# Chunk stores on GpSimd's queue, a first maximum pass over four banks, six x tiles turned among the sample batches, and a finer wait ahead of the feed-forward

## The chip, the cores and the metric

The kernel runs on one core of one Trainium2 chip. The metric is the device time of one execution in microseconds (us). The core has five engines with queues of their own: TensorE (PE: matmuls and transposes), VectorE (DVE), ScalarE (ACT), GpSimd (POOL) and SyncE (SP, which here only issues DMAs). They meet through semaphores.

## The reference

One layer over 1024 prompt tokens and 8 sample batches of 16 tokens (T = 1152 tokens in all), float32:

```python
D_MODEL, SEQ, DEC_BATCH, DEC_SEQ, PAST_LEN = 1024, 1024, 8, 16, 256
H_A, DH_A, H_B, DK_B, DV_B, D_FF, CONV_W, PLE_DIM = 8, 64, 4, 128, 256, 2816, 3, 256
def trunk_layer(x, p, fox_past, ...):
    qa, ka, va, fa, qb, kb, vb, rb, a1, ga, gb = split(x @ w_in)
    logf = log_sigmoid(fa + b_fgate)
    ya = fox(qa, ka, va, cumsum(logf), fox_past) @ w_a_out       # causal softmax attention, 8 heads
    la = log_sigmoid(a1 @ w_a2 + b_a2) / 16
    ob, S = gated_linear_attention(qb * DK_B**-0.5, kb, vb, la, S0)       # 4 heads
    yb = (rms_norm(ob) * g_gla * silu(rb)) @ w_b_out
    x1 = layer_norm(ALPHA * x + (sigmoid(ga) * ya + sigmoid(gb) * yb) @ w_o)
    val, gate = split(causal_conv3(x1 @ w_up))
    x2 = layer_norm(ALPHA * x1 + (val * gelu(gate)) @ w_down)
    return layer_norm(ALPHA * x2 + (p @ w_pl) * sigmoid(x2 @ w_plg)), ka, va, logf, S, conv_new
```

The sample batches attend to their 256 past keys and values and to their own 16 tokens.

## The kernel before

All large products are exact to about float32: each operand is split into a rounded part (`_hi`, by ACT) and a rest (`_lo`, by DVE), and a product is three matmuls (`split3`). Code is written out per engine; the order on each queue is that of the code. The stages that the change touches, in order of time:

**Projection.** x is transposed by TensorE into `xh`/`xl` (keys `("xT", n)`, nine tiles of 128 tokens), and q, k and v of branch A are computed. Weights pass through a ring of four slots (`load` on SP, `split_hi`, `split_lo`). Chunks 12 to 15 are the first four of branch B: `qb`, `kb` and two of `rb`, of head 0. Memory of `xh`/`xl` is then reused by branch A, so x has to be loaded and transposed again for branch B (`xs2`, keys `("xT2", n)`, `x_again`, `x_hi`, `x_lo`).

**Branch A, prompt.** Each of 8 heads has a first pass, `row_scores` and `row_max` (12 row blocks: scores by TensorE, maximum by DVE's reduction), then `join_max`, a transpose `turn_max` and ACT's `max_row`, which put the row maximum into an operand. The second pass has 6 slots a head (t counts them: 6 h + s): `scores(t)`, ACT's exp and rounding, DVE's `probs_lo`, and `probs_v(t - 2)` on TensorE. The first pass of head h + 1 runs among slots 0 to 3 of head h, `turn_max(h + 1)` in slot 4; only head 0's stands alone. The first pass has two half banks of PSUM (`n % 2`). Operands of a head are put together by 8 DMAs from SP (`head_operands`, 256 KB most of them), in three sets. A head gives two output chunks: ACT's `chunk_out(h, c)` copies one from PSUM to the single tile `ost`, `store_chunk(h, c)` writes it (`branch_a`, 128 KB) and the row sums (`row_sums`, 2 KB) to DRAM, and the next `chunk_out` waits until both have landed. In the queues of before, `store_chunk` is SP's, in order with `head_operands`, the loads of past keys and values (`past`) and `x_again`. POOL scales finished pairs of heads: `row_sums`, `row_scales`, `load_pair`, `store_pair` (a 128x1024 multiply).

**Branch A, samples.** For b in 0 to 10 TensorE does `past_keys(b + 1)`, `sample_out(b - 3)`, `sample_scores(b)`, `sample_turn(b - 1)` and `sample_v(b - 2)`. PSUM is handed out in turn by `take`: four buffers, and each use waits until the use four places earlier is drained. Then come the nine `xT2` transposes, and branch B with `thirds(("qb", 0), ...)`: 3 products (g = 0, 1, 2) over 384 tokens each, 24 matmuls a product.

**Ahead of the feed-forward.** The products with `w_o` (L924) alternate with transposes of finished x1 tiles (`turn_x1`, L912). DVE does for each tile the residual (`add_x`), `stats`, `centred`, `x1_scaled`, and `x1_lo`, which drains the PSUM buffer of the transpose. TensorE then waits at

```python
            copied(pe, ("wo", 1, NT - 1), ("x1T", NT - 3))
```

and starts `first_chunk`: six products of `w_up`, with `turn_x1(7)` and `turn_x1(8)` between them.

Of the kernel before, what the change touches and what calls it, by code (L numbers as in the profile page):

```python
# [24 lines left out]
P = 128  # L25
# [63 lines left out]
def build(nc, x_prompt, x_sample, cache_fox_k, cache_fox_v, cache_fox_logf, state_gla, cache_ffn_conv,  # L89
# [4 lines left out]
    with ctx:  # L94
# [121 lines left out]
        def x_tile(x, n):  # L216
# [21 lines left out]
        xs2 = [at(off["va"] + 1024 * i, 1024) for i in range(4)] + [at(off["kT"] + T * i, 1024) for i in range(4)] \  # L238
            + [at(off["qT"], 1024)]
# [25 lines left out]
        rbb = [at(off["kT"] + T, 1024)] * 3 + [at(off["e0"], 1024)]  # L265
# [311 lines left out]
        def _(pe):  # L577
# [13 lines left out]
            def thirds(key, chunk, x, kt=KT, lhs=None, first=None):  # L591

                w = weights(pe, chunk) if lhs is None else lhs
                for g in range(3):
# [5 lines left out]
                if chunk is not None:  # L600
                    w_last[chunk] = (*key, 2)
# [78 lines left out]
            def row_scores(h, u):  # L680
# [10 lines left out]
                o, t = bank[:, n % 2, 0:b - a], slice(i * P, (i + 1) * P)  # L691
# [62 lines left out]


# [54 lines left out]

            for n in range(NT):
                pe.wait_ge(s_xt[n], 32)
                turn_x("xT2", n, xs2[n])
# [4 lines left out]
            for h in range(H_B):  # L818
                thirds(("qb", h), ("qb", h), x_parts)
# [108 lines left out]
            copied(pe, ("wo", 1, NT - 1), ("x1T", NT - 3))  # L928
# [38 lines left out]
            def first_chunk():  # L967
# [4 lines left out]
                assert [turn[k] % 4 for k in (("wo", 1, NT - 1), ("x1T", 6), ("x1T", 7), ("x1T", 8))] == [0, 1, 2, 3]  # L972
                up(0, 0, 1, 0)
# [60 lines left out]
        def _(act):  # L1034
# [21 lines left out]
            def x_hi(key):  # L1056
                for n in range(NT):
# [4 lines left out]
            x_hi("xT")  # L1062
# [55 lines left out]
            for q in range(2):  # L1118
# [8 lines left out]
                if q == 0:  # L1127
                    split_hi(12)
# [3 lines left out]
            v_hi(0)  # L1132
            max_row(0)
            for t in range(NT_S + 2):
                h, s = divmod(t, NS)
                if t < NT_S:
# [14 lines left out]
                    if t == 1:  # L1151
                        qk_hi(1)
# [6 lines left out]

            split_hi(13)  # L1160
# [27 lines left out]
            copied(act, *[("soT", b) for b in range(DEC_B)], *[("spv", b) for b in range(DEC_B)])  # L1188
            split_hi(14)
            act.wait_ge(s_oao, 64)  # L1190
            act.wait_ge(s_oas2, 32 * 2 * H_A + 16)
            x_hi("xT2")
# [197 lines left out]
        def _(dve):  # L1390
# [30 lines left out]
            x_lo("xT", 0)  # L1421
# [43 lines left out]
            split_lo(12)  # L1465
# [853 lines left out]
```

## Time and profile before

| | |
|---|---|
| time, median of 3 runs | 2480.12 us (2478.81 to 2480.16) |
| profiled execution, its own time | 2480.29 us |
| span of its trace | 2478.6 us |
| TensorE busy | 2338.6 us, 94% |
| granted TensorE clock, mean | 0.973 of full |

All times of rows are us from the span's start unless marked ns. A matmul's shape is weights' partitions * columns, then the moving operand. A number in square brackets behind a row is how long the engine had been idle, and what released it. In a table of stretches the TensorE clock is the share of full speed (1.00 is 2.4 GHz, 0.50 is 1.2 GHz).

### The profile page before, as it was taken

How to read it: one execution, taken by the hardware profiler on the slowest of the kernel's cores; microseconds unless marked ns; L12 is line 12 of the kernel's file. 1: busy time of each engine (PE TensorE's matmuls, PEld its weight loads, DVE VectorE, ACT ScalarE, POOL GpSimd, SP SyncE). 2: the span in 40 equal slices, each digit the busy share in tenths (PEclk: the TensorE clock that was granted, in tenths of full speed). 3: DMA queues.
4: the chain of work that ended last, by engine and by line, in shares of the span. 5: the costliest groups of instructions: out<-in, count | busy, mean ns of one | idle time of the engine just before them, and what ended most of it. 6: DMA issues, size and time to landing. Idle time of an engine off the chain costs nothing.

```text
span 2478.6 us, 31985 instructions
## 1 busy us (share of the span) xinstructions
PE 2338.6 (94%) x13127; PEld 2148.3 (87%) x13127; DVE 1279.3 (52%) x1695; ACT 672.7 (27%) x1077; POOL 256.2 (10%) x441
## 2 busy tenths in 40 slices
PE   7999999898989898999999989999999999998797
PEld 6997776697989798999999879999999999997685
DVE  4124662354544545000443456766776766766685
ACT  3113663242424232211222133122122122221210
POOL 0001012001010101000022121000000000000421
PEclk8998999999999999999999999999999999999798
DMA  5125654111112120311313201111011111111210
GB/s 138 43 82 147 150 142 156 49 35 56 52 48 60 32 75 20 114 41 33 120 41 106 98 21 49 43 35 51 31 47 43 34 51 43 34 43 53 95 43 34
DMA packets 154399, 160.28 MB, mean 65 GB/s; under 512 B 13898, under 2 KB 126982, under 8 KB 153126
## 3 DMA queue, kind: packets, MB, share of 16 engines
q1 hardware_dynamic: 145878, 126.58, 17.4%
q0 software_dynamic: 8416, 32.20, 3.7%
q8 instruction: 79, 1.29, 0.2%
q14 instruction: 26, 0.21, 0.0%
HBM read 122.26 MB, written 23.84 MB: 59 GB/s over the span
## 4 chain that ended last, share of the span: by engine, by line
PE 88%; DVE 4%; issue 2%; ACT 2%; DMA 2%; SPq 1%; POOL 1%; DVEq 0%; ACTq 0%; POOLq 0%
PE ps L582 74%; PE ps L924 3%; PE ps L845 2%; PE ps L733 2%; PE ps L693 1%; DVE sb L1400 1%; DMA ring_raw<-in_w_in 1%; DVE sb L1488 1%; PE ps L715 1%; DMA row_sums<-sb 1%; PE ps L716 1%; PE ps L694 0%; PE ps L892 0%; DVE ring_lo L1410 0%; DVE sb L1833 0%
## 5 line engine op out<-in xcount | busy, mean ns | idle before, releaser
L582 PE MATMUL ps<-x_hi,up_hi 128*128 128x384 f32 x1056 | 354.6, 336 | 7.1 <-issue 7.1
L1044 ACT ACTIVATE sb<-ps 128x384 f32<-128x384 f32 (+6 forms) x312 | 128.7, 435 | 832.8 <-PE ps L582 769.1
L582 PE MATMUL ps<-x_hi,up_lo 128*128 128x384 f32 x1056 | 354.5, 336 | 0.0
L582 PE MATMUL ps<-x_lo,up_hi 128*128 128x384 f32 x1056 | 354.1, 335 | 0.0
L1833 DVE TENSOR_TENSOR sb<-sb,ps 128x512 f32<-128x512 f32 x396 | 270.9, 688 | 117.4 <-PE ps L582 117.0
L582 PE MATMUL ps<-x_hi,ring_hi 128*128 128x384 f32 x960 | 322.8, 336 | 3.4 <-DVE x_lo L1417 3.4
L582 PE MATMUL ps<-x_hi,ring_lo 128*128 128x384 f32 x960 | 321.4, 335 | 0.0
L582 PE MATMUL ps<-x_lo,ring_hi 128*128 128x384 f32 x960 | 321.4, 335 | 0.0
L1410 DVE TENSOR_TENSOR ring_lo<-ring_raw,ring_hi 128x1024 fp32r<-128x1024 f32 (+1 forms) x68 | 78.4, 1160 | 314.3 <-ACT ring_hi L1044 313.9
L582 PEld LDWEIGHTS ps<-x_hi,up_hi 128*128 128x128 f32 x1056 | 199.0, 188 | 9.7 <-issue 7.3
L582 PEld LDWEIGHTS ps<-x_lo,up_hi 128*128 128x128 f32 x1056 | 198.9, 188 | 2.5
L582 PEld LDWEIGHTS ps<-x_hi,up_lo 128*128 128x128 f32 x1056 | 198.9, 188 | 0.0
L582 PEld LDWEIGHTS ps<-x_hi,ring_hi 128*128 128x128 f32 x960 | 180.6, 188 | 5.9 <-DVE x_lo L1417 3.6
L582 PEld LDWEIGHTS ps<-x_lo,ring_hi 128*128 128x128 f32 x960 | 180.8, 188 | 0.1
L582 PEld LDWEIGHTS ps<-x_hi,ring_lo 128*128 128x128 f32 x960 | 180.7, 188 | 0.0
L582 PE MATMUL ps<-down_hi,h_hi 128*128 128x512 f32 x396 | 157.4, 397 | 4.4 <-DVE h_lo L1859 4.4
L582 PE MATMUL ps<-down_hi,h_lo 128*128 128x512 f32 x396 | 156.0, 394 | 0.0
L582 PE MATMUL ps<-down_lo,h_hi 128*128 128x512 f32 x396 | 155.7, 393 | 0.0
L1400 DVE SCALAR_TENSOR_TENSOR convolved_halves<-sb,convolved_halves 128x1168 f32<-128x1168 f32 x88 | 126.4, 1436 | 11.1 <-DVE convolved_halves L1822 1.4
L582 PE MATMUL ps<-ring_hi,x_hi 128*128 128x256 f32 x432 | 125.8, 291 | 0.0
L582 PE MATMUL ps<-sb 128*128 128x256 f32 (+4 forms) x400 | 106.5, 404 | 18.2 <-ACT sb L1253 14.3
L582 PE MATMUL ps<-ring_hi,x_lo 128*128 128x256 f32 x432 | 122.2, 283 | 0.0
(268 smaller groups left out, 4256.4 us busy)
## 6 DMA issues: line engine op xcount, KB each, us to landing
ring_raw<-in_w_in SPq DMA_DIRECT2D x52, 512.0 KB, 3.9
up_raw<-in_w_up SPq DMA_DIRECT2D x44, 512.0 KB, 4.0
sb<-in_x_prompt SPq DMA_DIRECT2D x24, 512.0 KB, 7.4
down_raw<-in_w_down SPq DMA_DIRECT2D x22, 512.0 KB, 4.6
branch_b<-sb POOLq DMA_DIRECT2D x4, 1152.0 KB, 7.9
ob_raw<-branch_b POOLq DMA_DIRECT2D x4, 1152.0 KB, 9.5
out<-sb POOLq DMA_DIRECT2D x9, 512.0 KB, 3.0
kk<-k_hi SPq DMA_DIRECT2D x16, 256.0 KB, 3.8
```

What stands on the lines that cost most here:

```text
L582: m = mm(out, l, r, start=(n == 0), stop=(n == len(pairs) - 1))
L693: mm(o, qq[:, t], kk[:, a:b], start=True, stop=False)
L715: mm(o, kk[:, k], qq[:, a:b], start=True, stop=False)
L716: m = mm(o, kc[0:KC, k], qc[0:KC, a:b], start=False, stop=not diag)
L733: m = mm(o, v[:, j, :], p[:, x], start=(j == n == 0), stop=(j == 4 * c + 3 and n == 2), skip_group_check=True)
L845: m = mm(o[:, t], a[:, t], c[:, t], start=True, stop=True)
L924: m = mm(o[:, 0:512], a, b, start=(k == i == 0), stop=(k == KT - 1 and i == 2))
L1044: return act.activation(out, in_, ACT.Copy, scale=scale)
L1400: return dve.scalar_tensor_tensor(out=out, in0=in0, scalar=scalar, in1=in1, op0=op0, op1=op1)
L1410: dve.tensor_tensor(ringl[:, i, 0:kt], ring[:, i, 0:kt], ringh[:, i, 0:kt].bitcast(F32), ALU.subtract)\
L1488: dve.tensor_reduce(mparts[:, c, i:i + 1], bank[:, n % 2, 0:b - a], AX.X, ALU.max).then_inc(s_mx, 1)
L1833: dve.tensor_tensor(z, z, bank[:, 4 + b, :], ALU.add).then_inc(dn_free[b], 1)
```

## The change

Six edits:

1. `store_chunk` moves from SP's queue to POOL's. POOL's steps on the pairs are laid out between the 16 chunk stores; `store_pair(j)` now stands behind `store_chunk(2 j + 3, 1)`. `row_sums(3)` and the first two `sample_queries` are moved accordingly, and the samples' output store is POOL's too.
2. Head 0's first pass goes over four half banks (`row_bank`), and six row blocks of head 1 are put around `turn_max(0)`, where before they stood in slots 0 and 1. `qk_hi(1)` and `qk_lo(1)` stand ahead of slot 0 rather than in slot 1.
3. Six of the nine `xT2` transposes stand in sample batches 0 to 5, in the order 6, 7, 8, 3, 4, 5; the x tiles have new homes.
4. Two of the three products of `qb` of head 0 (g = 2 and 1) stand in batches 8 and 9.
5. To make room for it, past keys 4 to 7 are loaded to the weights' ring two heads into branch A rather than at head 6, and weight chunks 12 and 13 are loaded and split behind them, in the samples, rather than ahead of branch A. `om`, `sP`, `sPT`, `oas` have other places.
6. Ahead of the feed-forward the wait for `("x1T", NT - 3)` is moved behind `turn_x1(NT - 1)`.

```diff
@@ PE
+        def row_bank(n):
+            return n % 4 if n < NR else n % 2
...
-                    if h:
+                    if h >= 2:
                         pe.wait_ge(s_mrow, h)
-                if n >= 2:
-                    pe.wait_ge(s_mx, n - 1)
+                if n >= 4:
+                    pe.wait_ge(s_mx, n - (3 if n < NR else 1))
...
             for u in range(NR):
                 row_scores(0, u)
+            for u in range(3):
+                row_scores(1, u)
             turn_max(0)
+            for u in range(3, 6):
+                row_scores(1, u)
             for t in range(NT_S + 2):
...
-                        if s < 4:
+                        if s < 4 and t >= 2:
...
             for b in range(DEC_B + 3):
...
+                if b < 6:
+                    turn_again(TURN_X2[b])
                 if b < DEC_B:
                     sample_scores(b)
                 if 1 <= b <= DEC_B:
                     sample_turn(b - 1)
+                if b in QB_EARLY:
+                    g = QB_EARLY[b]
+                    copied(pe, *[("xT2", n) for n in range(3 * g, 3 * g + 3)])
+                    thirds(("qb", 0), ("qb", 0), x_parts, only=(g,))
...
-            copied(pe, ("wo", 1, NT - 1), ("x1T", NT - 3))
+            copied(pe, ("wo", 1, NT - 1))
...
                 turn_x1(NT - 1)
+                copied(pe, ("x1T", NT - 3))
                 up(0, 0, 1, 0)
@@ ACT
             v_hi(0)
+            qk_hi(1)
             max_row(0)
...
+                if b < 6:
+                    x_hi("xT2", TURN_X2[b])
+                if b == DEC_B:
+                    split_hi(12, 13)
@@ DVE
             join_max(0)
+            for u in range(6):
+                row_max(1, u)
             v_lo(0)
+            qk_lo(1)
@@ POOL
+            for h in range(H_A):
+                store_chunk(h, 0)
+                if h and h % 2 == 0:
+                    row_sums(h // 2 - 1)
+                if h > 1 and h % 2 == 1:
...
+                    load_pair(h // 2 - 1)
...
+                store_chunk(h, 1)
+                if h and h % 2 == 0:
+                    row_scales(h // 2 - 1)
...
+                if h > 1 and h % 2 == 1:
+                    store_pair(h // 2 - 1)
@@ SP
-                if g:
-                    store_chunk(g - 1, 1)
-                store_chunk(g, 0)
```

What this does to the queues is shown at three places. First SP's queue of before, at the end of head 0; `head_operands(3)` is the group of L2165, past values are L2187, `store_chunk(0, 1)` the first pair of L2182 and L2183:

```order
L2165 DMA qq_68<-q_hi 64x1024 [waits scores_full,qk_lo_ready]
L2165 DMA kk_69<-k_hi 64x1024 x2
L2165 DMA qc_70<-q_hi 64x1024
L2165 DMA qq_68<-q_lo_61 64x1024
L2165 DMA kc_71<-k_lo_65 64x1024
L2165 DMA kc_71<-negC_r 1x16x64 x2
L2187 DMA sb<-in_cache_fox_v 128x2x512 [waits psum_full3]
L2187 DMA sb<-in_cache_fox_v 128x2x512 x3
L2182 DMA branch_a<-sb 64x512 [waits branch_a_chunk_ready]
L2183 DMA row_sums<-sb 1x512
```

And POOL's queue of the change, from `store_chunk(3, 0)` to `store_chunk(4, 0)`; L1984 is the multiply of `store_pair(0)`:

```order
L1991 DMA branch_a<-sb 64x512 [waits branch_a_chunk_ready]
L1992 DMA row_sums<-sb 16x1x32
L1977 DMA sb<-branch_a 128x1024 [waits row_sums_in,operands_in0,operands_in2]
L1979 DMA sb<-row_scales 64x1024 x2
L1991 DMA branch_a<-sb 64x512 [waits branch_a_chunk_ready]
L1992 DMA row_sums<-sb 16x1x32
L1984 ISA
L1984 TENSOR_TENSOR sb<-sb 128x1024 [waits row_sums_in]
L1986 DMA branch_a<-sb 128x1024 [waits branch_a_scaled]
L1991 DMA branch_a<-sb 64x512 [waits branch_a_chunk_ready]
```

The stores now stand behind POOL's own steps on the pairs instead of behind SP's loads.

The second place is TensorE's queue around `turn_max(0)`. Before (L702 is `turn_max`, L715 `scores(0)`, L693 `row_scores`):

```order
L693 MATMUL ps<-kk_69,qq_68 128x512 [waits part_max_or_x1_centred]
L694 MATMUL ps<-kc_71,qc_70 128x512
L696 MATMUL ps<-causal_r,identity_r 128x128
L702 MATMUL ps<-sb,m_hi_lo 2x128 [waits max_lo_ready]
L702 MATMUL ps<-sb,m_hi_lo 2x128 x7
L715 MATMUL ps<-qq_68,kk_69 128x512 [waits max_row_ready]
```

With the change (L709 is `turn_max`, L722 `scores(0)`, L700 `row_scores`; kk_73 and qq_72 are head 1's):

```order
L700 MATMUL ps<-kk_73,qq_72 128x384 [waits part_max_or_x1_centred]
L701 MATMUL ps<-kc_75,qc_74 128x384
L703 MATMUL ps<-causal_r,identity_r 128x128
L709 MATMUL ps<-sb,m_hi_lo 2x128 [waits max_lo_ready]
L709 MATMUL ps<-sb,m_hi_lo 2x128 x7
L700 MATMUL ps<-kk_73,qq_72 128x512 [waits part_max_or_x1_centred]
L701 MATMUL ps<-kc_75,qc_74 128x512
L703 MATMUL ps<-causal_r,identity_r 128x128
L700 MATMUL ps<-kk_73,qq_72 128x512 [waits part_max_or_x1_centred]
L701 MATMUL ps<-kc_75,qc_74 128x512
L700 MATMUL ps<-kk_73,qq_72 128x128 [waits part_max_or_x1_centred]
L722 MATMUL ps<-qq_68,kk_69 128x512 [waits max_row_ready]
```

Row blocks of head 1 now stand on both sides of `turn_max(0)`, where before nothing stood between it and `scores(0)`.

The third place is TensorE's queue where the samples end. With the change (L589 on x_hi and ring_hi is the first matmul of a product of `qb`, L621 an `xT2` transpose, L806 `sample_out`):

```order
L589 MATMUL ps<-x_hi,ring_hi 128x384 [waits weights_lo_ready,psum_free1,psum_free3]
L589 MATMUL ps<-sb 128x512 [waits psum_free2,psum_free1,v_past_in3]
L589 MATMUL ps<-sb 128x512 x2
L806 MATMUL ps<-sb 128x16 [waits psum_free3,psum_free2]
L806 MATMUL ps<-sb 128x16 x3
L621 MATMUL ps<-sb 128x128 [waits psum_free0,x_or_embedding_gate_in0]
L621 MATMUL ps<-sb 128x128 x7
L621 MATMUL ps<-sb 128x128 [waits psum_free1,x_or_embedding_gate_in1]
L621 MATMUL ps<-sb 128x128 x7
L621 MATMUL ps<-sb 128x128 [waits psum_free2,x_or_embedding_gate_in2]
L589 MATMUL ps<-x_hi,ring_hi 128x384 [waits gla_small_in,decay_rank_ready,psum_free3,weights_lo_ready,psum_free2,psum_free1,psum_free0]
```

Three `xT2` transposes are left behind the last `sample_out`, where there were nine, and one `qb` product where there were three.

## Rows read from the trace of the kernel before

**Rows 1.** The page: busy time, share and instructions by engine.
```profile
PE 2338.6 (94%) x13127; PEld 2148.3 (87%) x13127; DVE 1279.3 (52%) x1695; ACT 672.7 (27%) x1077; POOL 256.2 (10%) x441
```

**Rows 2.** Stretches of 4 us: busy by engine, PEclk, DMA share, GB/s.
```profile
268.00:272.00 4.00, 4.00 (x16) 3.31 (x15) 2.52 (x5) 1.87 (x2) 0.00 (x0) 0.50 1.00 209
...
392.00:396.00 4.00, 4.00 (x17) 3.05 (x16) 0.00 (x0) 1.38 (x2) 0.92 (x3) 0.79 0.92 315
```

**Rows 3.** The timeline, head 0's first pass: start, us, engine, line, operation.
```profile
214.13 0.69 DVE L1488 TENSOR_REDUCE sb<-ps 128x1 f32<-128x512 f32 x1 [0.85 <-PE ps L694]
216.44 1.87 PE L702 MATMUL ps<-sb,m_hi_lo 128*2 128x128 f32 x8 [1.39 <-DVE m_hi_lo L1400]
219.41 0.79 PE L715 MATMUL ps<-qq,kk 128*128 128x512 f32 x1 [1.10 <-ACT qc L1044]
221.38 0.41 PE L693 MATMUL ps<-kk,qq 128*128 128x128 f32 x1
227.62 0.73 PE L715 MATMUL ps<-qq,kk 128*128 128x512 f32 x1
236.51 0.42 PE L693 MATMUL ps<-kk,qq 128*128 128x384 f32 x1
```

**Rows 4.** The chain: `turn_max` of heads 1, 3 and 5 to 6.
```profile
240.20 0.87 PE ps L702 x8
...
285.10 0.87 PE ps L702 x8
...
326.01 0.87 PE ps L702 x8
...
345.64 0.87 PE ps L702 x8
```

**Rows 5.** The timeline, the store of chunk (0, 1) and what waits.
```profile
251.28 0.60 ACT L1044 ACTIVATE sb<-ps 65x512 f32<-65x512 f32 x1 [1.41 <-PE ps L733]
254.88 0.49 SPq L2182 DMA_DIRECT2D branch_a<-sb  x1
263.16 0.59 ACT L1044 ACTIVATE sb<-ps 65x512 f32<-65x512 f32 x1 [2.19 <-DMA row_sums<-sb]
266.63 0.50 PE L715 MATMUL ps<-qq,kk 128*128 128x512 f32 x1 [2.50 <-ACT qc L1044]
```

**Rows 6.** The timeline, the store of chunk (6, 1), and POOL beside it.
```profile
379.37 0.54 POOL L1946 DMA_DIRECT2D sb<-branch_a  x1 [4.80 <-DMA row_scales<-sb]
381.60 0.59 ACT L1044 ACTIVATE sb<-ps 65x512 f32<-65x512 f32 x1 [3.38 <-DMA row_sums<-sb]
385.16 0.69 PE L733 MATMUL ps<-p_hi,v_hi 128*65 128x512 f32 x1 [4.02 <-DVE p_lo L1501]
```

**Rows 7.** POOL's multiply, and DVE's `v_lo` beside it.
```profile
305.24 2.68 POOL L1953 TENSOR_TENSOR sb<-sb 128x1024 f32<-128x1024 f32 x1 [5.45 <-DMA sb<-row_scales]
305.56 2.90 DVE L1478 TENSOR_TENSOR v_lo<-sb,v_hi 128x512 fp32r<-128x512 f32 x1
```

**Rows 8.** The timeline, end of the samples and the `xT2` transposes.
```profile
466.67 3.69 PE L614 MATMUL ps<-sb 128*128 128x128 f32 x32
470.98 10.27 DVE L1417 TENSOR_TENSOR x_lo<-ps,x_hi 128x1024 fp32r<-128x1024 f32 x9 [1.45 <-ACT x_hi L1044]
472.35 5.59 PE L614 MATMUL ps<-sb 128*128 128x128 f32 x40 [1.99 <-DVE x_lo L1417]
481.31 0.45 PE L582 MATMUL ps<-x_hi,ring_hi 128*128 128x384 f32 x1 [3.37 <-DVE x_lo L1417]
```

**Rows 9.** The timelines of TensorE and of DVE ahead of the feed-forward.
```profile
1464.15 0.66 PE L582 MATMUL ps<-x_hi,up_hi 128*128 128x384 f32 x1 [7.08 <-issue]
1470.57 1.04 PE L912 MATMUL ps<-sb 128*128 128x128 f32 x8
1458.68 2.48 DVE L1400 SCALAR_TENSOR_TENSOR sb<-sb 128x1024 f32<-128x1024 f32 x2
1462.83 1.22 DVE L1766 TENSOR_TENSOR x_lo<-ps,x_hi 128x1024 fp32r<-128x1024 f32 x1
```

More of the change, by code:

```diff
@@ L589, in split_chain, with thirds @@
                 return chain(out, pairs)
-            def thirds(key, chunk, x, kt=KT, lhs=None, first=None):
+            def thirds(key, chunk, x, kt=KT, lhs=None, first=None, only=range(3)):
                 w = weights(pe, chunk) if lhs is None else lhs
-                for g in range(3):
+                for g in only:
                     if first is not None and key[-1] == 0:
@@ L1054, in split_hi, with x_hi @@
                         copy(ringh[:, n % W_SLOTS, 0:kt], ring[:, n % W_SLOTS, 0:kt]).then_inc(s_rh, 1)
-            def x_hi(key):
-                for n in range(NT):
+            def x_hi(key, *tiles):
+                for n in tiles:
                     o = product(act, (key, n))
@@ L1061, in _ @@
             act.wait_ge(s_const, 16)
-            x_hi("xT")
+            x_hi("xT", *range(NT))
             o = product(act, "cacheT")
@@ L1185, in _, with qb_third @@
                                    accum_out=rs[:, b % 2:b % 2 + 1]).then_inc(s_exs, 1)
-            copied(act, *[("soT", b) for b in range(DEC_B)], *[("spv", b) for b in range(DEC_B)])
+            def qb_third(h, g):
+                o = product(act, ("qb", h, g))
+                copy(qb[:, g * THIRD:(g + 1) * THIRD], o[:, 0:THIRD], DK ** -0.5).then_inc(drained(("qb", h, g)), 1)
+            qb_third(0, 2)
             split_hi(14)
+            qb_third(0, 1)
+            copied(act, *[("spv", b) for b in range(DEC_B)])
+            x_hi("xT2", *TURN_X2[6:])
+            copied(act, *[("soT", b) for b in range(DEC_B)])
             act.wait_ge(s_oao, 64)
             act.wait_ge(s_oas2, 32 * 2 * H_A + 16)
-            x_hi("xT2")
             copy(a1T, a1s).then_inc(s_a1, 1)
@@ L1201, in _ @@
             for h in range(H_B):
-                for g in range(3):
-                    o = product(act, ("qb", h, g))
-                    copy(qb[:, g * THIRD:(g + 1) * THIRD], o[:, 0:THIRD], DK ** -0.5).then_inc(drained(("qb", h, g)), 1)
+                for g in (range(3) if h else (0,)):
+                    qb_third(h, g)
                 m = 12 + 6 * h
@@ L1420, in _ @@
             dve.wait_ge(s_const, 16)
-            x_lo("xT", 0)
+            x_lo("xT", *range(NT))
             o = product(dve, "cwT")
@@ L1541, in _ @@
                         .then_inc(drained(("soT", b - 3)), 1)
+                if b < 6:
+                    x_lo("xT2", TURN_X2[b])
                 if b < DEC_B:
@@ L1567, in _ @@
             split_lo(14)
-            x_lo("xT2", 1)
+            x_lo("xT2", *TURN_X2[6:])
             dve.wait_ge(s_qbd, DEC_B)
@@ L2221, in _ @@
                         past(b, k_part)
-            store_chunk(H_A - 1, 1)
+                if g == 1:
+                    past_pe(sp, ("va", 1, NT - 1))
+                    for b in range(4):
+                        past(b, v_part)
+                if g == 2:
+                    for b in range(4, 8):
+                        past(b, k_part)
+            sp.wait_ge(s_s2, NS * (H_A - 1))
+            for b in range(4, 8):
+                past(b, v_part)
+            sp.wait_ge(s_vl, H_A)
+            sp.wait_ge(s_ov, 32)
+            x_again(6, 7, 8, 3)
             sp.wait_ge(s_pv, NT_S)
-            x_again(6, 7, 4, 8)
-            sp.wait_ge(s_oao, 48)
-            x_again(5)
+            x_again(4)
+            for n, after in ((5, 6), (0, 7), (1, 8), (2, 3)):
+                past_pe(sp, ("xT2", after))
+                x_again(n)
             past_pe(sp, ("spv", 3))
```

130 lines of the change are left out of this document (60 added, 70 removed).

## The prediction

> **What bounds the kernel now.** I read the page first: TensorE is busy for 94% of the span [rows 1]. So what can be won lies where it stands still, or where it is busy at half clock. The waits of TensorE and a table of its clock in stretches of 4 us show five such places in the parts that the diff touches. I then read the timeline around each, on all engines, to see what ended last.
>
> Place A, head 0's first pass: with two half banks TensorE and DVE take turns, then `turn_max` waits 1.39 us and `scores(0)` 1.10 us, and the clock falls to 1.2 GHz: eight transposes take 1.87 us where later ones take 0.87 [rows 3, 4]. Half clock lasts to 236.5.
>
> Place B, heads 1 and 2: the chain gives 44.90 us from `turn_max(1)` to `turn_max(3)`, but 19.63 us for a head once it is steady (326.01 to 345.64) [rows 4]. What is late is ACT: its copy of chunk (0, 1) was done at 251.88, SP issued the store only at 254.88, behind its loads, and ACT could copy the next chunk only at 263.16; TensorE then stood for 2.50 us and ran at half clock [rows 2, 5].
>
> Place C: 285.10 to 326.01 is 1.65 us more than two steady heads [rows 4]. There DVE's `v_lo` takes 2.90 us and ends as POOL's multiply does [rows 7]; an instruction of twice its width takes 1.22 us [rows 9].
>
> Place D, end of branch A's prompt: ACT waits 3.38 us for the store of chunk (6, 1), TensorE 4.02 us, and the clock is at 0.79 of full as late as 392 to 396 [rows 2, 6].
>
> Place E, the `xT2` transposes: from 466.67 to 481.31, 14.6 us, for 9.3 us of transposes; DVE's nine `x_lo` end last [rows 8].
>
> Place F: TensorE waits 7.08 us for the drain of x1T(6). The profile names no releaser, but the wait ends as DVE's `x1_lo(6)` does, at 1464.05, which stands behind `x1_scaled(8)` [rows 9].
>
> **The change, part by part.** The sum is made against the profiled execution's own 2480.3 us, which is 0.2 above the median of the runs.
>
> *F, the finer wait.* `up(0, 0, 0, 0)` needs tiles 0 to 2 and the drain of wo(1, 8) alone. It can start at 1457.2. Before, this product took from 1464.15 to 1470.57, 6.4 us, since the wait had cost the clock; with no wait the clock stays, and 24 matmuls at full clock take 4.2 (an estimate: 24 x 0.174, the distance of such matmuls behind 1469). The next thing, `turn_x1(7)`, needs x1_scaled(7), done at 1461.16 [rows 9], and would come at 1461.4, so it waits for nothing. The moved wait needs 1464.05 and is reached after 1467. Gain 1470.6 - 1461.4 = 9.2. Bounds: 7.0 (if the clock falls anyway) and 9.3.
>
> *B, stores on POOL's queue.* POOL is idle there, so the store of (0, 1) is issued at once. Two DMAs cost it about 1.1 us (0.54 each [rows 6]). How long they land beside SP's loads is not shown for this tile; the nearest row is a store of 8 KB from POOL's queue under full load, whose successor waited 4.80 us [rows 6]. 251.88 + 1.1 + 5 = 258, and ACT is ready for the next copy at 260.97 (263.16 - 2.19). So the stall goes, with its half clock. The excess is 44.90 - 2 x 19.63 = 5.6; I leave 0.4 for ACT's rounding of q and k that also stands there. Gain 5.2; bounds 0 and 5.6.
>
> *C, where the multiply falls.* `store_pair(0)` now comes behind chunk (3, 1), in slot 1 of head 4, where DVE has one `p_lo` to be held, by at most the multiply's 2.7 us, less what it has already run: I take 0.4 lost. The excess of 1.65 goes. Gain 1.3; bounds -1.5 (two multiplies that hold TensorE in full slots) and 1.7.
>
> *D.* The same move, but here all of SP's loads (4 MB) are in flight and the heads' slots are short. The 8 KB store issued at 374.0 beside it landed by 379.4 [rows 6]. With 1.1 us of issue and about the same landing, chunk (6, 1) lands at 379.8 rather than 381.6. Gain 1.8 at ACT, and TensorE's wait of 4.02 becomes 2.2. Whether the clock then falls decides another 4.0: it is half from 384 to about 394.5, in which TensorE works some 8.5 us that would take half as long, less a little for the copies behind it. A wait of 2.50 us did cost the clock [rows 2, 5], one of 1.99 did not [rows 8]. 2.2 is nearer to the second. I take 5.8; bounds 0 and 6.
>
> *A, first pass.* DVE's reduction of 512 columns takes 0.69 us [rows 3]; there are six of these and six shorter ones, 6.8 us in all (estimate by columns). With four banks DVE runs them without gaps and joins by 214 (before, the last block was reduced at 215.8, one behind the row at 214.13). But the block of head 1 just ahead of `turn_max(0)` waits for a bank whose reduction stands behind the join, so `turn_max(0)` comes at about 215.3 (before: 216.44). In between TensorE has little to do for 3 us, less than where the clock fell before, so I take half clock again: `turn_max` 1.9, three blocks 2.2, and `scores(0)` at 219.3, as before (219.41). What is gained is behind it: six row blocks are done. They took 221.38 to 227.62, less 1.3 for slot 1's scores: 5.0 us at half clock [rows 3]. And ACT's and DVE's work for `qk_hi(1)`, `qk_lo(1)` has left slot 1, whose delay of a row block and of `probs_v(0)` was about 1 us. So the point that stood at 236.51 is reached at 230.5. Gain 6.0. Without the fall of the clock it would be 10; at worst 4, if half clock lasts 4 us longer. Head 1's operands are needed at 212.8 rather than at 221.38 [rows 3]; their last DMA is issued at 209, so a wait of some tenths can come. SP's loads (two weight chunks gone from ahead, past keys 4 to 7 now at head 2) lie beside the heads and cost nothing while each head's operands still land in the half head that they have.
>
> *E, transposes and `qb`.* A transpose tile is 3.69/4 = 0.92 us of TensorE, `x_lo` 10.27/9 = 1.14 [rows 8]. Behind the last `sample_out` three remain: 0.95 to the first, 1.0 for its `x_hi`, three `x_lo`, 5.4 us instead of 14.6. The path of the samples' output store, now POOL's (copy 0.3, issue and landing up to 5, ACT's copy of a1 1.2), is 4.5 to 6.7 and may end last by about 1. The samples are full on TensorE, so six transposes there cost their 5.5 us. One more PSUM use in a batch changes whose buffer is taken over: in batch 2 the transpose takes that of `sample_scores(1)`, which DVE frees some 2.4 us after it is full; 1.0 us. The two `qb` products cost there what they save later. ACT's and DVE's work in batches (1.0 and 1.1 us more in nine) is covered by `sample_scores`' 4 us. Gain 14.6 - 5.4 - 5.5 - 1.0 = 2.7; bounds 1 and 5 (with a clock that stays up behind it).
>
> **Sum.** 9.2 + 5.2 + 1.3 + 5.8 + 6.0 + 2.7 = 30.2. 2480.3 - 30.2 = **2450** us.
>
> **The rivals.** *D's clock falls all the same* (the wait is 2.5 or more, as where it fell in B): 4.0 less, 2454. *A keeps its clock*: its gain is 10, 2446. For it: TensorE's first 12 blocks are denser than before; against it: the thin stretch at 211.4 to 214.6.
>
> *The stores land no earlier.* Their bytes share 16 DMA engines with SP's loads, whose traffic is at a share of 1.00 in 268 to 272 [rows 2]. In D the landing time then stays at 381.6, and in B, where 3 us of SP's delay go but the landing would be 9 or more, ACT would still be late. B and D are lost, 11.0: 2461. Against it: the 8 KB store in D landed 2 us before SP's, issued at the same time [rows 6].
>
> The Trainium skill, DMA: Bandwidth & Descriptors, "Issuing engines are not separate DMA queues", says that transfers started by any engine run on the same 16 engines and interleave, so that another queue saves issue time alone; by it the time would be 2461. The same page's "Queues, rings and completion order" has each engine go round between the queues packet by packet, which would let a store pass the loads in front of it. The trace fits the second better, by the 2 us above.
>
> *POOL's queue becomes the hold (slower).* A store that stands behind a blocked step of POOL, or lands later from this queue, stops ACT in every head. Between chunk (h, 1) and (h + 1, 0) there are about 7 us in a steady head; issue 1.1 and landing 5 leave 1. From 6 us of landing on, each of seven heads loses what exceeds it, and from a TensorE wait of 2.5 its clock too (3 us): at 9 us of landing 7 x 6 = 42 us are lost against 30 won, 2492. For it: the landing of 4.8 under load; against it: that row is from the fullest stretch of all, and POOL's multiply (2.7 us) ends 3 us before the next chunk.
>
> **Chances.** Forecast as written, each term near its value, 0.45; D's clock falls 0.22; A keeps its clock (with or without D) 0.12; stores no earlier 0.15; POOL holds 0.03; a change with no effect (the six gains eaten by waits that I do not see) 0.03. The range reaches from all clocks up (2442) to the stores' rival (2461). By over 0.2% (5 us), about what can be told from no change: faster 0.95, within 0.02, slower 0.03.
>
> **What the profile will show.** F: no wait above 0.5 us between the last `w_o` product and the feed-forward, clock 1.00 there. B: 39 to 40 us between `turn_max(1)` and `turn_max(3)`. D: a TensorE wait of 2.0 to 2.5 us ahead of the last `probs_v`. A: slot 3's scores done 6 us earlier, clock at half at 216 to 230. E: 5 to 6.5 us from the last `sample_out` to `qb`. I am wrong if POOL's stores take over 6 us to land, or if the samples lose more than 7 us to the six transposes.

## The result, and the profile after

The changed kernel takes 2452.0 us, the median of 4 runs (2451.4 to 2452.3); the kernel before, run beside it, 2479.8 us. The ratio is 0.9888, with a 95% interval of 0.9871 to 0.9905: 28 us are won, where 30 were forecast. Of the six terms one was 5 us too low, and two were 3 and 2 us too high. The profiled execution has a span of 2450.3 us, that of before 2478.6.

The page, busy time by engine. TensorE does the same work in 14 us less busy time, since less of it runs at half clock; the other 14 us were waits [rows 1].

```profile
PE 2324.6 (95%) x13127; PEld 2138.9 (87%) x13127; DVE 1276.1 (52%) x1695; ACT 672.2 (27%) x1077; POOL 273.1 (11%) x474
```

The table sets the two traces side by side at the same instructions of TensorE, by their starts in the timeline. "Won" is the difference of the two stretches.

| stretch | before | after | won | forecast |
|---|---|---|---|---|
| span's start to the first row block | 206.06 | 207.65 | -1.6 | 0 |
| to turn_max(1): A | 33.98 | 22.55 | 11.4 | 6.0 |
| to turn_max(3): B | 44.89 | 39.75 | 5.1 | 5.2 |
| to turn_max(7): C | 80.15 | 79.00 | 1.15 | 1.3 |
| to past_keys(0): D | 24.27 | 21.72 | 2.55 | 5.8 |
| to the first `la` product: E | 118.74 | 118.13 | 0.6 | 2.7 |
| to the first level product | 32.68 | 34.23 | -1.55 | 0 |
| to turn_x1(6) | 915.25 | 914.68 | 0.6 | 0 |
| to turn_x1(7): F | 14.55 | 5.40 | 9.15 | 9.2 |
| to the span's end | 8.0 | 7.2 | 0.8 | 0 |

The last row is of the time behind turn_x1(7), less 1000 us that are the same: 1008.0 and 1007.2.

Stretches of 4 us after (columns: busy time of TensorE, its weight loads, DVE, ACT and POOL, granted clock, DMA share, GB/s). The clock is at 1.00 in 216 to 220 and 268 to 272, where it was 0.50 [rows 2]. It falls in three other places.

```profile
216.00:220.00 4.00, 3.74 (x26) 2.98 (x24) 3.10 (x6) 2.52 (x3) 0.00 (x0) 1.00 0.67 201
...
268.00:272.00 4.00, 4.00 (x29) 3.14 (x29) 3.27 (x7) 3.64 (x5) 1.61 (x3) 1.00 0.64 218
368.00:372.00 4.00, 3.27 (x18) 2.84 (x17) 0.00 (x0) 0.59 (x1) 2.63 (x8) 0.57 1.00 259
...
468.00:472.00 4.00, 2.10 (x7) 2.13 (x8) 0.34 (x1) 1.16 (x1) 2.98 (x3) 0.50 0.23 42
...
492.00:496.00 4.00, 4.00 (x17) 4.00 (x16) 1.22 (x1) 3.95 (x4) 0.00 (x0) 0.64 0.02 5
```

The chain after, `turn_max` of heads 1, 3, 5 and 6: 39.75 us from head 1 to head 3, and 39.74 from 3 to 5, so both are at the steady pace of 2 x 19.64 but for 0.5 us [rows 4].

```profile
230.36 0.87 PE ps L709 x8
270.11 0.87 PE ps L709 x8
309.85 0.87 PE ps L709 x8
329.49 0.87 PE ps L709 x8
```

The timelines after, in this order: head 0's `turn_max`, now at full clock (1.04 us for 1.87) and with no wait in brackets [rows 3]; ACT's copy of chunk (1, 0) and TensorE's `scores` that had waited 2.50 us for it [rows 5]; the store of chunk (6, 1), ACT's next copy and the `probs_v` behind it [rows 6].

```profile
215.78 1.04 PE L709 MATMUL ps<-sb,m_hi_lo 128*2 128x128 f32 x8
...
251.03 0.57 ACT L1063 ACTIVATE sb<-ps 65x512 f32<-65x512 f32 x1
254.48 0.50 PE L722 MATMUL ps<-qq,kk 128*128 128x512 f32 x1 [0.20 <-ACT qc L1063]
...
358.64 0.50 POOL L1992 DMA_DIRECT2D row_sums<-sb  x1
363.87 0.59 ACT L1063 ACTIVATE sb<-ps 65x512 f32<-65x512 f32 x1 [1.78 <-DMA row_sums<-sb]
367.43 0.44 PE L740 MATMUL ps<-p_hi,v_hi 128*65 128x512 f32 x1 [2.43 <-DVE p_lo L1527]
```

Chunk (0, 1)'s store no longer holds ACT. That of (6, 1) still does, for 1.78 us: its row sums were issued at 358.64 and landed at 363.8, 5.2 us later. TensorE waits 2.43 us, and the clock falls.

The end of the samples after, and the way to F. POOL's store was issued at 463.53 and let its next instruction go at 468.32, 4.8 us later. ACT's copy of a1, which waits for this store, ends at 469.54, and `qb` starts 7.36 us behind the first of the last transposes [rows 8]. In F, `turn_x1` 6, 7 and 8 come 5.4 and 5.1 us apart, with no wait, where the product behind 6 had waited 7.08 [rows 9].

```profile
462.54 2.82 PE L621 MATMUL ps<-sb 128*128 128x128 f32 x24
463.53 0.75 POOL L2036 DMA_DIRECT2D branch_a<-sb  x1 [41.51 <-DVE sb L1569]
464.85 3.49 DVE L1444 TENSOR_TENSOR x_lo<-ps,x_hi 128x1024 fp32r<-128x1024 f32 x3 [0.48 <-ACT x_hi L1063]
468.32 1.06 POOL L2042 MEMSET sb<- 128x1152 f32 x1 [4.04 <-DMA branch_a<-sb]
468.38 1.16 ACT L1063 ACTIVATE sb<-sb 16x1152 f32<-16x1152 f32 x1 [1.80 <-DVE x_lo L1444]
469.90 0.66 PE L589 MATMUL ps<-x_hi,ring_hi 128*128 128x384 f32 x1 [4.55 <-ACT sb L1063]
...
1437.71 1.04 PE L930 MATMUL ps<-sb 128*128 128x128 f32 x8
1443.11 1.04 PE L930 MATMUL ps<-sb 128*128 128x128 f32 x8
1448.17 1.03 PE L930 MATMUL ps<-sb 128*128 128x128 f32 x8
```

### The profile page after: what moved, and what is told of

Its sections match the earlier page's. It is cut to its first block, busy times and chain, and to the rows that moved or that the text cites. A ratio compares the mean times of both kernels' runs of the same rounds, so it can differ in the third digit from the quotient of the medians.

```text
span 2450.3 us, 31995 instructions
## 1 busy us (share of the span) xinstructions
PE 2324.6 (95%) x13127; PEld 2138.9 (87%) x13127; DVE 1276.1 (52%) x1695; ACT 672.2 (27%) x1077; POOL 273.1 (11%) x474
## 4 chain that ended last, share of the span: by engine, by line
PE 89%; DVE 4%; ACT 2%; issue 2%; DMA 1%; POOL 1%; SPq 1%; DVEq 0%; ACTq 0%; POOLq 0%
PE ps L589 75%; PE ps L942 3%; PE ps L863 2%; PE ps L740 2%; DVE sb L1514 1%; PE ps L700 1%; DMA ring_raw<-in_w_in 1%; DVE sb L1424 1%; PE ps L722 1%; PE ps L723 1%; POOL plg_lo L2134 0%; PE ps L910 0%; POOL sb L2057 0%; PE ps L701 0%; ACT ring_hi L1063 0%
## 5 line engine op out<-in xcount | busy, mean ns | idle before, releaser
L589 PE MATMUL ps<-x_hi,up_hi 128*128 128x384 f32 x1056 | 353.7, 335 | 0.1
L589 PE MATMUL ps<-x_hi,up_lo 128*128 128x384 f32 x1056 | 353.7, 335 | 0.0
L589 PE MATMUL ps<-x_lo,up_hi 128*128 128x384 f32 x1056 | 353.2, 334 | 0.0
L589 PE MATMUL ps<-x_hi,ring_hi 128*128 128x384 f32 x960 | 323.9, 337 | 4.8 <-ACT sb L1063 4.5
L589 PE MATMUL ps<-x_lo,ring_hi 128*128 128x384 f32 x960 | 322.2, 336 | 0.0
L589 PE MATMUL ps<-x_hi,ring_lo 128*128 128x384 f32 x960 | 322.1, 336 | 0.0
L589 PEld LDWEIGHTS ps<-x_hi,up_hi 128*128 128x128 f32 x1056 | 198.2, 188 | 2.8 <-DVE sb L1424 0.3
L589 PEld LDWEIGHTS ps<-x_lo,up_hi 128*128 128x128 f32 x1056 | 198.2, 188 | 2.5
L589 PEld LDWEIGHTS ps<-x_hi,up_lo 128*128 128x128 f32 x1056 | 198.2, 188 | 0.0
L589 PEld LDWEIGHTS ps<-x_hi,ring_hi 128*128 128x128 f32 x960 | 181.4, 189 | 7.6 <-issue 7.4
L589 PEld LDWEIGHTS ps<-x_lo,ring_hi 128*128 128x128 f32 x960 | 181.5, 189 | 0.1
L589 PEld LDWEIGHTS ps<-x_hi,ring_lo 128*128 128x128 f32 x960 | 181.3, 189 | 0.0
L589 PE MATMUL ps<-down_hi,h_hi 128*128 128x512 f32 x396 | 157.1, 397 | 4.4 <-DVE h_lo L1890 4.4
L589 PE MATMUL ps<-down_hi,h_lo 128*128 128x512 f32 x396 | 155.8, 394 | 0.0
L589 PE MATMUL ps<-down_lo,h_hi 128*128 128x512 f32 x396 | 155.5, 393 | 0.0
L589 PE MATMUL ps<-ring_hi,x_hi 128*128 128x256 f32 x432 | 125.8, 291 | 0.0
L589 PE MATMUL ps<-ring_hi,x_lo 128*128 128x256 f32 x432 | 122.2, 283 | 0.0
L589 PE MATMUL ps<-ring_lo,x_hi 128*128 128x256 f32 x432 | 122.1, 283 | 0.0
```

The lines of the kernel that those rows point to most:

```text
L589: m = mm(out, l, r, start=(n == 0), stop=(n == len(pairs) - 1))
```

## The experiments

Each starts from the changed kernel. What a run says is read at the same instructions as in the table above, since the medians of one kernel move by 1 to 2 us, and its single runs by 1 to 5, in blocks_back and in the kernel before by 7 to 9.

### The changed kernel once more

> The changed kernel itself, once more, beside all_three on the same chip. It is to tell how far one kernel's profile and times move from chip to chip and run to run, by which the other runs are read. Theory (the start, 206 to 208 us up to the first row block, moves by 1 to 2 us and is no part of the change; the second fall of the clock, near 492, belongs to the kernel): 2452 us, the fall is there again. Rival (the second fall is an accident of one execution): the clock is 1.00 there, and the span is 1.5 us shorter.

Measured: 2451.2 us (2449.8 to 2452.0), span 2448.1; the first row block at 205.92, and 22.53 us from there to turn_max(1). The start moves by 1.7 us between two executions of one kernel (205.85 to 208.14 over all the kernels here), so the -1.6 of the table is no part of the change. The second fall is there again:

```profile
488.00:492.00 4.00, 4.00 (x15) 3.61 (x14) 1.22 (x1) 3.90 (x5) 0.00 (x0) 0.65 0.41 123
```

### A: what kept the clock

`two_banks`:

```diff
-            return n % 4 if n < NR else n % 2
+            return n % 2
...
-                if n >= 4:
-                    pe.wait_ge(s_mx, n - (3 if n < NR else 1))
+                if n >= 2:
+                    pe.wait_ge(s_mx, n - 1)
```

> The changed kernel with head 0's first pass back on two half banks; the six row blocks of head 1 stay ahead of the slots. It is to tell what kept the clock in place A, which was at 1.00 all through 200 to 368 where I had forecast half clock up to 230. Theory 1 (the four banks kept it, since TensorE no longer takes turns with DVE): the clock falls again near 216, turn_max(0) comes about 1 us later at half clock, and all of slot 0 to 3 up to about 236 runs slow: 5 to 6 us lost, 2457.5 us. Theory 2 (the row blocks around turn_max kept it): the clock stays at 1.00 and only DVE's later join costs, 1 to 1.5 us, 2453.3 us.

`blocks_back`:

```diff
-            for u in range(3):
-                row_scores(1, u)
             turn_max(0)
-            for u in range(3, 6):
-                row_scores(1, u)
...
-                        if s < 4 and t >= 2:
+                        if s < 4:
```

(and the same for DVE's six reductions)

> The changed kernel with the six row blocks of head 1 back in slots 0 and 1; head 0's first pass keeps its four banks, and ACT's and DVE's rounding of the next q and k keeps its new place. Theory 1 (the four banks kept the clock): it stays at 1.00, and what is lost is the filling of TensorE's wait for the last maximum, 3 to 4 us: 2455.5 us. Theory 2 (the row blocks around turn_max kept it): the clock falls as before the change, 5 us more are lost: 2460.5 us, turn_max(0) at twice its time.

Measured: two_banks 2453.2 us (2451.8 to 2455.1), blocks_back 2453.2 (2449.9 to 2457.2). From the first row block to turn_max(1): 22.55 us in the changed kernel, 24.74 with two banks, 29.81 with the blocks back, 33.98 before. The stretches of 4 us, first two_banks, then blocks_back:

```profile
216.00:220.00 4.00, 3.30 (x23) 2.59 (x22) 2.69 (x8) 0.42 (x1) 0.00 (x0) 1.00 0.87 270
```

```profile
212.00:216.00 4.00, 1.30 (x9) 0.86 (x10) 3.90 (x8) 2.15 (x3) 0.00 (x0) 1.00 1.04 370
216.00:220.00 4.00, 4.00 (x17) 3.85 (x16) 1.22 (x4) 2.85 (x3) 0.00 (x0) 0.51 0.97 211
```

With two banks the clock stays; with the blocks back TensorE is busy for 1.30 of 4 us around `turn_max(0)`, and the clock is at half from 216 to about 233. In the profiled executions theory 2 holds: 7.3 us are lost without the row blocks, and 2.2 us without the second pair of banks.

But blocks_back does not lose its clock every time. Its four runs fall into two pairs, 2449.9 twice and 2456.5 and 2457.2, with mean granted clocks of 0.979 and 0.980 in the first pair and 0.976 in both of the second. A difference of 0.003 to 0.004 over 2450 us is some 15 to 20 us more at half clock (an estimate), and the profile, which is of the second pair, has 17. The first pair is as fast as the changed kernel. So what the row blocks win is the clock; where it stays without them, these runs show nothing won.

The kernel before adds a second doubt. Its clock fell at 212.8, late in the first pass and ahead of both waits that the prediction put the fall down to. Two_banks has the same matmuls up to there, with the same waits, and passes at full clock. The stretch of 4 us and a row of the timeline, in the kernel before and in two_banks; the two rows are the same matmul, at half clock and at full:

```profile
212.00:216.00 4.00, 2.68 (x9) 1.80 (x7) 2.70 (x5) 0.00 (x0) 0.00 (x0) 0.60 1.04 368
212.87 0.80 PE L693 MATMUL ps<-kk,qq 128*128 128x512 f32 x1 [0.37 <-DVE sb L1488]
```

```profile
212.00:216.00 4.00, 3.14 (x15) 2.34 (x15) 2.51 (x6) 2.01 (x2) 0.00 (x0) 1.00 0.92 330
214.93 0.50 PE L700 MATMUL ps<-kk,qq 128*128 128x512 f32 x1 [0.37 <-DVE sb L1514]
```

So the row blocks keep the clock where blocks_back loses it, behind `turn_max(0)`. Why it fell earlier than that in the kernel before stays open.

### B, C, D: whose queue

`stores_on_sp`: `store_chunk` is SP's again, `store_chunk(g - 1, 1)` and `store_chunk(g, 0)` behind head g's loads (at the last head also behind past values and four of the x tiles):

```diff
-                store_chunk(h, 0)        # in POOL's loop, and store_chunk(h, 1)
...
+                if g:                    # in SP's loop
+                    store_chunk(g - 1, 1)
+                store_chunk(g, 0)
```

> The changed kernel with the chunk stores back on SP's queue, behind the loads that stand there; POOL keeps its new order of the pair steps, and SP the new order of its loads. Theory (POOL's queue, which issues at once, is what B and D gained by): turn_max(1) to turn_max(3) goes from 39.75 back to 44 or 45 us, ACT waits 2 us or more for the store of chunk (0, 1), TensorE's wait ahead of the last probs_v goes from 2.43 to about 4; 6 to 7 us lost, 2458.7 us. Rival (the order of the loads did it, and a queue of its own saves nothing): within 1 us of 2452.

Measured: 2460.4 us (2456.9 to 2461.2). turn_max(1) to turn_max(3) takes 43.69 us (39.75), turn_max(3) to turn_max(7) 80.15 (79.00, and 80.15 before), TensorE's wait ahead of the last probs_v 4.06. So 7.0 us are lost up to past_keys(0): 3.9 in B, 1.15 in C and 1.95 in D. The timelines of ACT, POOL and DVE:

```profile
252.91 0.59 ACT L1063 ACTIVATE sb<-ps 65x512 f32<-65x512 f32 x1 [2.31 <-DMA row_sums<-sb]
293.73 2.62 POOL L1984 TENSOR_TENSOR sb<-sb 128x1024 f32<-128x1024 f32 x1 [5.10 <-DMA sb<-row_scales]
294.00 2.90 DVE L1504 TENSOR_TENSOR v_lo<-sb,v_hi 128x512 fp32r<-128x512 f32 x1
```

The rival is out. In this run SP issued the store of chunk (0, 1) at 244.75, 3.2 us behind ACT's copy, where POOL had issued it within 0.3 us. The last two rows show term C too: without the chunk's store ahead of it POOL multiplies 9.65 us earlier, on top of `v_lo`, which takes 2.90 us; in the changed kernel `v_lo` takes 0.69.

`spare_buffer`: chunk (6, 1) is copied to 512 free columns in place of the one buffer:

```diff
+        osts = [ost] * 16
+        osts[13] = at(off["kT"] + 2 * T, 512)
...
-                if h + c:
+                if h + c and 2 * h + c != 14:
                     act.wait_ge(s_oas2, 32 * (2 * h + c))
...
```

> The changed kernel with a buffer of its own for chunk (6, 1), so that ACT's copy of chunk (7, 0) waits for no store. Theory (this wait of 1.8 us at ACT makes TensorE's wait of 2.4 us ahead of the last probs_v, and that the half clock behind it): the wait falls to 0.6 us or less, the clock stays at 1.00 in 368 to 376; 1.8 + 2.2 = 4 us won, 2448 us. Rival (in the short last slots the exponentials and their rounding take as long by themselves): TensorE still waits 1.5 us or more, below 1 us won, 2451.3 us.

Measured: 2445.2 us (2443.5 to 2448.9). From turn_max(7) to past_keys(0) 19.28 us (21.72), and 2.4 us less from there to `la`. TensorE's wait, and the clock behind it:

```profile
364.27 0.44 PE L742 MATMUL ps<-p_hi,v_hi 128*65 128x512 f32 x1 [0.54 <-DVE p_lo L1529]
```

```profile
364.00:368.00 4.00, 3.00 (x22) 2.48 (x23) 0.69 (x2) 0.62 (x2) 3.80 (x10) 1.00 0.82 233
368.00:372.00 4.00, 4.00 (x27) 3.24 (x25) 0.97 (x1) 2.85 (x3) 2.07 (x2) 1.00 0.86 242
```

The theory holds: the wait is 0.54, the clock stays, and 4.8 us are won by the profile up to `la`. The second fall is absent too (1.5 us), which brings this near the 6.8 us between the medians.

### E: transposes, the store, and the wait ahead of qb

`no_transposes`: edit E undone (x tiles turned behind the samples, all three thirds of `qb` there, and the buffers of the x tiles and the samples in their old places):

```diff
-                if b < 6:
-                    turn_again(TURN_X2[b])
...
-            for n in TURN_X2[6:]:
+            for n in range(NT):
                 turn_again(n)
```

> The changed kernel without edit E: the nine transposes of x and all of qb stand behind the sample batches again, as in the kernel before; first pass, stores, pair steps, finer wait and the order of the weight loads stay. Theory (E was worth nearly nothing: 0.6 us up to the first la product, and a second fall of the clock behind it took 1.5 us back): within 1.5 us of the changed kernel, 2451.1 us, and the clock is 1.00 through the first la product, as before. Rival (E gave its forecast of 2.7, and what I see behind it belongs to something else): 2454.7 us, with the second fall still there.

Measured: 2454.2 us (2451.6 to 2456.9); past_keys(0) to `la` takes 122.60 us, 4.5 more than in the changed kernel and 3.9 more than before; the clock is 1.00 behind `la`. Most of the 3.9 stands on ACT's timeline: in this order x_hi waits for the samples' store, which POOL issued beside SP's loads:

```profile
454.36 3.77 ACT L1061 ACTIVATE x_hi<-ps 128x1024 fp32r<-128x1024 f32 x4 [13.53 <-DMA branch_a<-sb]
```

ACT starts 7.0 us behind the last `sample_out`, before 4.1. The store's landing takes 5.2 us from its issue here, where before ACT went on 2.7 us behind the issue. So this run is no clean control for E: it has the store in the new queue and the old dependence on it, and shows that its new place costs some 2.9 us where something waits for it. By the time it is at the rival (2454.7), by the clock behind `la` with the theory.

`samples_store_sp`: the same store on SP's queue, ahead of its loads:

```diff
-            pool.dma_start(oa_out[:, :, SEQ:T], oas).then_inc(s_oas2, 16)
...
+            sp.dma_start(oa_out[:, :, SEQ:T], oas).then_inc(s_ov, 16)
```

> The changed kernel with the samples' output store issued by SP again, ahead of SP's two loads, instead of by POOL beside them. Theory (its landing, 4.7 us beside 0.6 MB of loads, is what ends the 7.36 us between the last sample_out and qb): ACT's copy of a1 comes about 1.4 us earlier, qb at x_lo's end, 6 us behind sample_out; 1.0 us won, 2451.0 us. Rival (the two loads, which now stand behind it, end last in its place): within 0.5 us of 2452.

Measured: 2448.5 us (2448.1 to 2450.3); `sample_out` to qb takes 7.01 us (8.28). The timelines:

```profile
465.39 1.16 ACT L1063 ACTIVATE sb<-sb 16x1152 f32<-16x1152 f32 x1
467.42 0.66 PE L589 MATMUL ps<-x_hi,ring_hi 128*128 128x384 f32 x1 [3.28 <-DVE x_lo L1446]
```

ACT's copy waits for nothing and DVE's `x_lo` ends last: 1.3 us at this place, where the theory had 1.0. The rest of the 3.5 us between the medians comes from other places of the profile. The second fall is absent here (1.5), and so is the fall at the end of branch A's prompt (2.3 in the samples); against them, turn_max(1) to turn_max(3) takes 42.02 us for 39.75, since ACT's rounding of q waits 2.18 us for the DMAs of a head's operands. Why these differ from the changed kernel was not tested.

`fill_wait`:

```diff
-        QB_EARLY = {DEC_B: 2, DEC_B + 1: 1}
+        QB_EARLY = {DEC_B: 2}
...
             for n in TURN_X2[6:]:
                 turn_again(n)
+            thirds(("qb", 0), ("qb", 0), x_parts, only=(1,))
```

> The changed kernel with the product qb of the tiles 3 to 5 moved from sample batch 9 to behind the last three transposes, where TensorE waits 4.55 us. Theory (the wait is filled by 4.2 us of work that depends on nothing late, and with no wait of over 2 us the clock stays up there and behind the la product): the wait goes below 1 us, the clock is 1.00 at 464 to 496; 4.2 + 1.5 + 1.5 = 7 us won, 2445 us. Rival (in batch 9 the product covered a wait of the last sample, which now shows): 0 to 2 us won, 2451 us.

Measured: 2443.7 us (2442.4 to 2445.5); past_keys(0) to `la` 109.71 us (118.13), `la` to the level product 32.69 (34.23). The waits of TensorE in 440 to 500 (total, times, longest), and its clock where the 4.55 us had been:

```profile
PE ps L589 <- ACT sb L1064: 0.5, 1, 0.5
```

```profile
460.00:464.00 4.00, 3.52 (x21) 3.23 (x20) 1.41 (x2) 1.66 (x2) 2.48 (x3) 1.00 0.16 63
```

Of these 8.4 us, 1.4 are only moved: the fall of the clock at the end of branch A's prompt lies earlier here, so turn_max(7) to past_keys(0) takes 23.09 us for 21.72. From turn_max(7) to `la` it is 132.80 for 139.85, 7.1 us won, and the second fall, absent here, is 1.5 more. The theory holds, and batch 9 had lost nothing by being emptied: the same product that cost 4.2 us there is nearly free in the wait.

### F: the wait put back

```diff
-            copied(pe, ("wo", 1, NT - 1))
+            copied(pe, ("wo", 1, NT - 1), ("x1T", NT - 3))
...
-                copied(pe, ("x1T", NT - 3))
```

> The changed kernel with the wait for the drain of x1T(6) back ahead of the feed-forward. Theory (this wait was all of place F): TensorE waits 7 us there, runs at half clock behind it, 9.2 us lost, 2461.2 us. Rival (with the work before it earlier, DVE's chain is shorter or another wait takes part of it): 3 to 6 us lost, 2456.5 us.

Measured: 2460.3 us (2459.7 to 2461.7); turn_x1(6) to turn_x1(7) 14.52 us for 5.40, so 9.1 us:

```profile
1444.23 0.66 PE L589 MATMUL ps<-x_hi,up_hi 128*128 128x384 f32 x1 [7.10 <-issue]
```

### The versions that beat both

> The changed kernel with the three edits that won time one by one: the product of tiles 3 to 5 behind the last transposes, a buffer of its own for chunk (6, 1), and the samples' output store on SP's queue ahead of its loads. Theory (they take away different waits, so they add): 8 for the first by its own profile, 4.5 for the second, up to 0.5 for the third, since the product now covers the wait that it shortened: 13 us won, 2439 us. Rival (with the clock kept at the first place, the half clock behind the second one comes back or a new one appears, as clock falls have moved between kernels here): 2443 us, no better than the first edit alone.

> all_three without the move of the samples' output store: the product of tiles 3 to 5 behind the last transposes and a buffer of its own for chunk (6, 1). Theory (the product covers what the store's landing cost, 0.5 us of wait is left): within 0.6 us of all_three, 2439.5 us. Rival (the landing still ends last there): 1.3 us above all_three, 2440.3 us, with a wait of over 1 us ahead of qb's last third.

Measured: all_three 2442.1 us (2439.5 to 2442.8), 0.9849 of before (0.9836 to 0.9862); fill_spare 2441.1 us (2439.4 to 2442.3), 0.9845 (0.9833 to 0.9858). Both are faster than the changed kernel beside them (2451.2) by 9 to 10 us and cannot be told apart. From turn_max(7) to `la` all_three takes 128.73 us, 4.1 less than fill_wait, so up to there the edits add as the theory has it. But the medians gain only 1.6 to 2.6 over fill_wait alone. That is nearer to the rival's 2443 than to 2439, and its reason stands in the traces, half clock at places where fill_wait has none. Fill_spare waits 0.83 us ahead of `qb`'s last third, so its own theory (the product covers the landing) holds. But its clock falls in the `qb` product of batch 8, behind waits of 0.84 and 0.29 us, and its samples take 1.6 us longer than those of all_three, which has the same waits there and keeps its clock:

```profile
440.00:444.00 4.00, 3.71 (x14) 3.50 (x13) 1.69 (x3) 0.49 (x1) 0.00 (x0) 0.58 0.00 0
```

The second fall is in all_three, though nothing there waits or runs slow ahead of it:

```profile
480.00:484.00 4.00, 4.00 (x18) 4.00 (x17) 1.22 (x1) 3.95 (x4) 0.00 (x0) 0.65 0.01 3
```

## Why the prediction was right, and where it was not

**F was right** in place and size: 9.15 for 9.2, with no wait of TensorE and full clock. wait_back takes 9.1 back. The step on which it rested, that the 7 us ended with DVE's `x1_lo(6)` though the profile names no releaser, is borne out: the wait on this drain alone was moved.

**B was right**: 5.1 for 5.2, 39.75 us from turn_max(1) to turn_max(3) where 39 to 40 were named. stores_on_sp gives 3.9 back, not all; the other 1.2 us were not separated; this run keeps the new order of SP's loads among other things. One sign of being wrong was named, a landing of over 6 us, and it came: the row sums of chunk (0, 1) took 6.2. They were there at 249.1, 1.9 us before ACT copied the next chunk, where the forecast had 3 us to spare. By the Trainium skill, DMA: Bandwidth & Descriptors, "Issuing engines are not separate DMA queues", another queue saves issue time alone; the forecast made 2461 us of it. The kernel with the stores back on SP takes 2460.4 and the changed kernel 2452.0, so the 8 us are there. But this does not refute the section: SP's issue behind its loads (3.2 us late in stores_on_sp) was itself the delay.

**C was right**, 1.15 for 1.3, and for the named reason: `v_lo` takes 0.69 us in place of 2.90, and goes back to 2.90 where the multiply does.

**D was mis-sized**: 2.55 for 5.8. The step on ACT was right: it waits 1.78 us for 3.38, where 1.6 was forecast, and TensorE 2.43, where 2.0 to 2.5 was named. The step that failed is "2.2 is nearer to the second. I take 5.8": the clock did fall, to 0.57 in 368 to 372. That was the first rival, priced at 1.8. That the fall was the missing part is shown best by two_banks, where this place is unchanged: its wait is 2.42 us, its clock stays, and turn_max(7) to the last `sample_out` takes 109.81 us for 112.67. So with the clock kept D comes to 5.4 of the 5.8, and which of the two prices is paid could not be read from the length of the wait.

**A was mis-sized the other way**: 11.4 for 6.0. `turn_max(0)` came 8.1 us behind the first row block where 9.2 was forecast. The step that failed is "so I take half clock again". I called the stretch around `turn_max(0)` thin, and it isn't: with three row blocks in it and three behind it TensorE is busy for 2.99 of 4 us in 212 to 216, against 1.30 in blocks_back, where the clock falls. The rival "A keeps its clock" was priced at 10. One reading under it was in the wrong order as well: `turn_max` and `scores(0)` did not wait first and lose the clock by it. It had fallen at 212.8, 3.7 us before `turn_max(0)` started.

**E was mis-sized**: 0.6 for 2.7, and 1.5 us given back behind it. The samples took 90.95 us from past_keys(0) to the last `sample_out`, before 76.40: 8.4 of the difference are two of `qb`'s products and 6.2 the six transposes, forecast 6.5. The failing step is the way out, taken at 5.4 us: it came out at 7.36, so 7.3 us were won and not 9.2. From the start of the last `sample_out` it is 8.28 us, where 5 to 6.5 was named and 15.56 stood before. Samples_store_sp divides the 2.0 us: with DVE's `x_lo` ending last it takes 6.10, which is 0.7 more than 5.4, and the output store adds the other 1.3. The prediction had seen that this store "may end last by about 1", but its sum left that out; issue and landing, 4.8 us, lie within the "up to 5" that it named. The half clock behind the wait of 4.55 us took 0.5 more than the one that stood there before. fill_wait removes wait and half clock and wins 7.1 us.

**The second fall of the clock** near the first `la` product (0.93 and 0.64 in 488 to 496, 1.55 us) was in no term. Its cause stays open. It is in both profiles of the changed kernel, in two_banks, blocks_back, stores_on_sp, wait_back and all_three, and not in the kernel before, no_transposes, samples_store_sp, spare_buffer, fill_wait and fill_spare; TensorE is busy for 4.00 of 4 us there in all of them, and in all seven traces the fall begins 2.6 to 3.2 us behind the start of the first `la` product. These are matmuls with weights of 16 partitions; the six traces without the fall have them too, and no run changes them. That it follows the fall ahead of `qb` by a fixed time is refuted by samples_store_sp and spare_buffer, which have that one and not this one, and by all_three, which has this one alone.

That the sum came within 2 us is thus partly luck: A's 5.4 too few and D's, E's and the second fall's 6.9 too many nearly cancel.

## What to carry to other kernels

Where an engine waits for something that can't come sooner, look for work that depends on nothing late and put it into the wait: here six row blocks gave 7.3 us in the execution in which the clock would have fallen without them, and one product of 4.2 us gave 7, since a filled wait can keep the clock as well as the time. Work moved out of a wait into a place where the engine was full is not won; ask of each moved piece whether it leaves a full place for an empty one. And before moving a store to an idle engine's queue ask what is issued beside it: behind another engine's loads it wins by its early issue (3 us of delay gone here), but beside loads that used to stand behind it, it lands later (4.7 us for 2.7).

## What the runs showed of the hardware

The length of TensorE's wait does not by itself decide whether its clock falls. At one place, ahead of the last probs_v, the clock fell with waits of 2.25 to 2.43 us in the changed kernel (both profiles), no_transposes, blocks_back and wait_back, and with 2.95 in fill_wait, while it stayed at 1.00 through 2.42 us in two_banks and 2.90 in samples_store_sp, whose stretches these are:

```profile
364.00:368.00 4.00, 2.19 (x13) 1.31 (x11) 0.59 (x2) 2.44 (x4) 1.58 (x3) 1.00 0.57 201
368.00:372.00 4.00, 2.18 (x14) 1.66 (x15) 1.50 (x2) 1.40 (x3) 3.26 (x10) 1.00 0.79 210
```

In fill_spare it fell behind waits of no more than 0.84 us, in the first pass of the kernel before behind waits of no more than 0.78, and to 0.64 and 0.65 in stretches in which TensorE was busy throughout (the second fall). So a term that rests on a clock that just stays or just falls has both its prices in the range, whichever is nearer.
